# The second FFN of a decoder step by seven block products, and two residuals moved from GpSimd to VectorE

## Chip, cores and metric

One NeuronCore of a Trainium2 chip runs the whole step in one launch. The metric is the device time of that core in microseconds. A median is over three runs of the same program.

## What is computed

One inference step of a one-layer decoder: 1024 prompt rows and 32 sample rows (8 sequences of 4), D = 1024, F = 2816, all in float32.

```python
h = x + 0.5 * rms_norm(swiglu_ffn(rms_norm(x, norms[0]), f1_gu, f1_d), norms[1])
mix = token_mixer(rms_norm(h, norms[2]), ...)
h = h + rms_norm(mix, norms[3])
h = h + 0.5 * rms_norm(swiglu_ffn(rms_norm(h, norms[4]), f2_gu, f2_d), norms[5])

def swiglu_ffn(x, w_gate_up, w_down):
    gate, up = jnp.split(x @ w_gate_up, 2, axis=-1)
    return (jax.nn.silu(gate) * up) @ w_down
```

The token mixer (gated DeltaNet heads and stick-breaking heads, then `@ w_o`) is in the middle and is not touched. The two FFNs have the same shapes.

## The kernel before

**Number format.** Every large product is made of three matmuls. An operand a is split into a_hi (ScalarE rounds it to fp32r) and a_lo = a - a_hi (VectorE); the product is hi*hi + lo*hi + hi*lo, accumulated in PSUM. So every operand costs a ScalarE pass and a VectorE pass, and three matmuls, beside what it costs to load.

**Order.** Each engine's instructions are written as generators that yield times; `interleave` merges them into one program order per engine. There is no other scheduler: an instruction that waits holds up everything behind it on its engine. The times are units of a stage's own (one is a mixing tile in `second_half`).

**First FFN, `Ffn7` (line 572).** The rows lie in two parts, q = 0 (2 x 256 rows) and q = 1 (2 x 272, with the sample rows). Tokens times weights is a 2 x 2 block product, done with seven products in place of eight, which needs sums of the token blocks (t1 to t4) and of the weight blocks (s1 to s4). Four stages:

- *Head* (`head_project`, L674): the first pair of 128 wide column blocks (gate and up), without the trick: 16 products of 24 matmuls. Beside it `TokenSplit` (L1320) turns the normed rows, writes hi, a raw copy and lo, and `sums_add`, `sums_hi`, `sums_lo` make the token sums.
- *Units* (`units`, L820): 20 units, one for each remaining column block, of seven products (L815 to L817) with 24 matmuls each, 256 or 272 columns wide. The results are chained by VectorE (`dve_unit`), the hidden values' sums are stored to DRAM (`hid_rows`, `store_hidden`), and the sample rows' down product is made on the way (L792).
- *Streamed down* (`down`, L1201): 7 products over the 11 pairs of hidden blocks. Six of them are 66 steps of 12 matmuls (L1219 to L1221). Step s needs a row of hidden sums, read back from DRAM into a ring of three (`load_a`, L1050: load s waits until a_lo of step s-3 is made), its hi and lo (L1106, L1119), and the hi and lo of a 128x512 block of w_down or of a sum of such blocks (L1113, L1121). w_down's quarters lie in four slots; `step_sums` (L1123) makes their sums from step 20 on and waits for the whole slot 12.
- *Last product* (`down_last`, L1181): the seventh product, by stripes i = 0 to 3 of 33 matmuls (L1193 to L1195). Stripe i waits for u3d, the additions of the sixth product (`down_adds`).

**Mixing and the seam (`second_half`, L2172).** For nine tiles, TensorE turns `mixed` (L2325) and multiplies by w_o in two halves a tile (L2337 to L2339) into banks 4 and 5; ScalarE evacuates (L2395) and squares (L2356), VectorE scales (L2502), GpSimd adds the residual h1 (L2306), ScalarE squares again, VectorE makes the normed row (L2506). SyncE stores h2 and loads the next h1.

**Second FFN, `Ffn` (line 125).** `Turn` (L465) turns the normed rows in three thirds of 352. `head_project` (L197) makes the first group of two column blocks in 12 products of 24 matmuls. Then ten groups g: gate and up of two column blocks, each 3 x 24 matmuls of 352 columns (L192 to L194), with the down product of group g-1 between them (L300 for the samples, L289 to L291, 96 matmuls of 512 columns), added to `mixed` by VectorE (L406). `down_last` (L337) is the last group's down product. Between its additions, for the tiles in turn, ScalarE squares (L2356), VectorE scales (L2521), GpSimd adds h2 (L2314) and SyncE stores; the last two tiles are VectorE's (L2527 to L2544).

## Time and profile before

| | us |
|---|---|
| median of three runs (2561.99 to 2565.17) | 2563.99 |
| the profiled execution, its own time | 2572.63 |
| its span | 2570.9 |

The profile is of one execution. Busy time is the union of an engine's instructions; PE is TensorE's matmuls, PEld its weight loads, DVE VectorE, ACT ScalarE, POOL GpSimd, SP SyncE. PEclk is the granted share of TensorE's full clock. A row of a view gives, behind a bar, the engine's idle time before the instruction and what ended it. Names with a_ belong to the first half of the kernel, with b_ to the token mixer, with c_ to the second half.

### The profile page before, as it was taken

Reading aid. Unit: us, or ns where it says so; the run is one execution under the profiler, and the core shown is the slowest. Engines: PE = TensorE matmul, PEld = TensorE weight load, DVE = VectorE, ACT = ScalarE, POOL = GpSimd, SP = SyncE. Lnnn points to the kernel's source line nnn. Section 1 sums busy time; section 2 is a strip of 40 time slices with the busy share of each in tenths; the row PEclk is TensorE's granted clock in tenths of the full one; section 3 lists DMA queues with packets and bytes.
Section 4 is the critical chain, followed back from the end, with each engine's and each line's share of the span. In section 5 each row is a group of like instructions: output and inputs, shape, how many; then the busy total and the mean of one; then the engine's idle time right before and its main releaser. Section 6 shows DMA issues by size and latency. Waiting matters only on the chain. (4 is left out here: it accounts for less than half of the span.)

```text
span 2570.9 us, 45774 instructions
## 1 busy us (share of the span) xinstructions
PE 2419.8 (94%) x18476; PEld 2140.8 (83%) x18476; DVE 1418.0 (55%) x2368; ACT 983.1 (38%) x1786; POOL 86.7 (3%) x125
## 2 busy tenths in 40 slices
PE   7999999999999899989788888799999999999997
PEld 7999999978788788878677755578999999999995
DVE  7767666658763675665357766445433333333335
ACT  7322222244545675657445545334211111111112
POOL 0000000000000000000110000021000000000002
PEclk9999999999999999999898989899999999999999
DMA  4433333464532122211286677431311111011113
GB/s 148 139 112 122 110 122 110 158 220 130 165 115 69 45 56 56 63 48 46 65 288 202 215 245 257 145 123 52 99 50 50 49 36 45 33 49 39 43 57 108
DMA packets 232611, 275.50 MB, mean 107 GB/s; under 512 B 15737, under 2 KB 160377, under 8 KB 232464
## 3 DMA queue, kind: packets, MB, share of 16 engines
q1 hardware_dynamic: 232464, 273.45, 33.1%
q8 instruction: 103, 1.69, 0.3%
q14 instruction: 44, 0.36, 0.0%
HBM read 222.51 MB, written 50.89 MB: 106 GB/s over the span
## 5 line engine op out<-in xcount | busy, mean ns | idle before, releaser
L1546 PE MATMUL a_q<-a_uh,a_p_hi 128*128 128x352 f32 x672 | 241.4, 359 | 0.0
L1548 PE MATMUL a_q<-a_uh,a_p_lo 128*128 128x352 f32 x672 | 219.1, 326 | 0.0
L1547 PE MATMUL a_q<-a_ul,a_p_hi 128*128 128x352 f32 x672 | 218.9, 326 | 0.0
L373 ACT ACTIVATE c_hid_hi<-c_hid 128x1056 fp32r<-128x1056 f32 x20 | 21.7, 1086 | 451.6 <-DVE c_hid_samples L262 451.6
L194 PE MATMUL c_q<-c_uh,c_lo_u 128*128 128x352 f32 x528 | 170.8, 323 | 0.0
L194 PE MATMUL c_q<-c_uh,c_lo_g 128*128 128x352 f32 x528 | 170.7, 323 | 0.0
L192 PE MATMUL c_q<-c_uh,c_hi_u 128*128 128x352 f32 x528 | 170.6, 323 | 0.0
L192 PE MATMUL c_q<-c_uh,c_hi_g 128*128 128x352 f32 x528 | 170.5, 323 | 0.0
L193 PE MATMUL c_q<-c_ul,c_hi_u 128*128 128x352 f32 x528 | 170.0, 322 | 0.0
L193 PE MATMUL c_q<-c_ul,c_hi_g 128*128 128x352 f32 x528 | 170.0, 322 | 0.0
L406 DVE TENSOR_TENSOR w_mixed<-w_mixed,c_q 128x512 f32<-128x512 f32 x160 | 109.4, 687 | 104.7 <-PE c_q L291 104.7
L1546 PEld LDWEIGHTS a_q<-a_uh,a_p_hi 128*128 128x128 f32 x672 | 129.1, 192 | 28.2 <-issue 24.4
L289 PE MATMUL c_q<-c_hi_d,c_hid_hi 128*128 128x512 f32 x352 | 141.2, 401 | 3.6 <-DVE w_mixed L406 3.6
L291 PE MATMUL c_q<-c_lo_d,c_hid_hi 128*128 128x512 f32 x352 | 138.9, 395 | 0.0
L290 PE MATMUL c_q<-c_hi_d,c_hid_lo 128*128 128x512 f32 x352 | 138.7, 394 | 0.0
L1547 PEld LDWEIGHTS a_q<-a_ul,a_p_hi 128*128 128x128 f32 x672 | 129.6, 193 | 0.0
L1548 PEld LDWEIGHTS a_q<-a_uh,a_p_lo 128*128 128x128 f32 x672 | 128.5, 191 | 0.0
L423 DVE TENSOR_TENSOR c_hid<-c_silu,c_q 128x352 f32<-128x352 f32 x60 | 31.3, 522 | 174.6 <-PE c_q L194 174.6
L1219 PE MATMUL a_q<-a_b_hi,a_a_hi 128*128 128x512 f32 x264 | 104.3, 395 | 3.3 <-DVE a_a_lo L1119 3.1
L1221 PE MATMUL a_q<-a_b_lo,a_a_hi 128*128 128x512 f32 x264 | 103.7, 393 | 0.0
L1220 PE MATMUL a_q<-a_b_hi,a_a_lo 128*128 128x512 f32 x264 | 103.5, 392 | 0.0
L194 PEld LDWEIGHTS c_q<-c_uh,c_lo_g 128*128 128x128 f32 x528 | 100.2, 190 | 0.0
(618 smaller groups left out, 6510.5 us busy)
## 6 DMA issues: line engine op xcount, KB each, us to landing
b_page<-in_cache_k SPq DMA_DIRECT2D x128, 256.0 KB, 3.7
b_page<-in_cache_v SPq DMA_DIRECT2D x128, 256.0 KB, 3.7
a_w_raw<-in_ffn_gu SPq DMA_DIRECT2D x44, 512.0 KB, 5.1
a_a_raw<-hid_rows SPq DMA_DIRECT2D x66, 256.0 KB, 2.7
a_p_raw<-in_w_in SPq DMA_DIRECT2D x28, 512.0 KB, 4.0
a_raw_d<-in_ffn_d SPq DMA_DIRECT2D x11, 1024.0 KB, 4.9
hid_rows<-a_hs SPq DMA_DIRECT2D x44, 256.0 KB, 3.4
c_raw_g<-in_ffn_gu SPq DMA_DIRECT2D x11, 1024.0 KB, 5.1
```

What stands on the lines that cost most here:

```text
L192: nc.tensor.matmul(out[:, 0:TB], wh, uh[:, c, :], start=(c == 0), stop=False)
L193: nc.tensor.matmul(out[:, 0:TB], wh, ul[:, c, :], start=False, stop=False)
L194: mm = nc.tensor.matmul(out[:, 0:TB], wl, uh[:, c, :], start=False, stop=(c == KC - 1))
L289: nc.tensor.matmul(bank, hh, wh, start=(e == 0), stop=False)
L290: nc.tensor.matmul(bank, hl, wh, start=False, stop=False)
L291: mm = nc.tensor.matmul(bank, hh, wl, start=False, stop=(e == 1))
L406: self.nc.vector.tensor_tensor(to, to, self.pd[at % 2], ALU.add).then_inc(self.E("added"), 1)
L1219: nc.tensor.matmul(out[i], ah[:, cols], bh[:], start=(k == 0), stop=False)
L1221: mm = nc.tensor.matmul(out[i], ah[:, cols], bl[:], start=False, stop=(k == PAIRS - 1))
L1546: nc.tensor.matmul(self.pm[at % 2][:, 0:TB], wh, self.uh[t][:, c], start=(c == 0), stop=False)
L1547: nc.tensor.matmul(self.pm[at % 2][:, 0:TB], wh, self.ul[t][:, c], start=False, stop=False)
L1548: mm = nc.tensor.matmul(self.pm[at % 2][:, 0:TB], wl, self.uh[t][:, c], start=False, stop=(c == KC - 1))
```

## The change

The class `Ffn` is removed, and the second FFN is made by the class of the first, `Ffn7`, with a layout of its own in `second_half`. The layout tells where buffers lie, after which head products the first unit's weight buffers are free (`first_free`), which banks the head uses (four: 0, 1, 4, 5; in the first FFN six), and which banks the last product uses (those of the fifth, so that it waits for the event v and not for u3d). `TokenSplit` takes the tiles in order 0 to 8 and gets waits of its own. The output norms follow as tiles become ready: the sample tile and tiles 0 to 3 during the down phase, 4 to 7 beside the last product, each with a VectorE multiplication by the gain (while ScalarE makes the root) and a fused multiply and add of the residual; GpSimd has no part in them. In the mixing, GpSimd adds the residual for tiles 0 to 6, and VectorE, in the same fused form, for tiles 7 and 8. Some order times change, and a few semaphores of the sample's delta rule are merged, with the same counts in the same order. The first FFN's program keeps its order.

```diff
...
-class Ffn:
...
+        self.first_free, self.head_banks, self.last_banks, self.last_freed = (lay[x] for x in ("first_free", "head_banks", "last_banks", "last_freed"))
...
+                    older = i - len(self.head_banks)
+                    if older >= 0:
+                        pe.wait_ge(E("hid0" if gu else "silu0"), older // 2 + 1)
                     wh, wl = self.w0[e][gu]
-                    out = self.bank[i % 6][:, 0:WQ[q]]
+                    out = self.head_bank(i)[:, 0:WQ[q]]
...
-                    pe.wait_ge(E("u3d"), i + 1)
+                    pe.wait_ge(E(self.last_freed), i + 1)
...
+        return [self.bank[b] for b in (self.last_banks if j == 6 else (0, 1, 4, 5) if j in (0, 2, 4) else (2, 3, 6, 7))]
...
-        f = Ffn(nc, s, "f2", f_map, uh, ul, y, bank, ffn_gu, ffn_d, 103424)
+        lay = {"head": lambda q, n, size: (H0 + 32768 * q + 2 * size * n, H0 + 32768 * q + 2 * size * n + size),
...
+               "first_raw": [M0 + 28672, M0 + 36864], "first_free": [13, 14, 15, 13, 16, 15, 16], "head_banks": bank[0:2] + bank[4:6],
...
+               "kept1": M0 + 49152, "last_banks": (0, 1, 4, 5), "last_freed": "v"}
+        f = Ffn7(nc, s, "f2", whole.at, lay, quad, bank, y, ffn_gu, ffn_d, hid_rows)
...
-        turn = Turn(nc, s, "n3", uh, ul, bank[6:8], ident, lambda i: mixed[:, i, :], E("hn_ready"),
-                    [-3, -2, -1, 0.5, 1.5, 2.5, 4.5, 5.5, 6.5])
+        first_pair, second_pair = bank[6:8], bank[2:4]
+        split = TokenSplit(nc, s, "n3", f, [second_pair if z % 2 else first_pair for z in range(N)], ident,
+                           lambda z: hn_last if z == NT else mixed[:, z, :], E("hn_ready"), list(range(N)),
+                           [-3.9, -3.2, -2.2, -1.5, 0.35, 1.2, 2.0, 2.8, 3.6])
...
-        LAST = [0, NT] + list(range(1, NT))
+        LAST = [NT] + list(range(NT))
         ALL = 2 * N
-        FFN_AT, FFN_UNIT = 9.0, 0.33
+        BY_POOL = NT - 1
+        FFN_AT, FFN_UNIT = 9.0, 0.268
+        FIRST_AT = (5.9, 6.3, 6.8, 7.3)
+        TAIL_AT = [-60, -31, -24, -15, -6, 4.4, 12.0, 19.6, 27.0]
...
-                sp.wait_ge(E("w_lo"), 2 * KC)
-                f.load(sp, "g", 0)
                 sp.wait_ge(sample.E("states_out"), 16 * H_DN)
-                f.load(sp, "u", 0)
+                for e in range(2):
+                    f.load_weights(sp, 0, e)
...
-            f.load(sp, "d", 0)
-            f.load_groups(sp)
...
+            f.load_weights(sp, 1, 0)
+            sp.wait_ge(f.E("mm0"), 14)
+            f.load_weights(sp, 1, 1)
+            f.load_units(sp)
+
+            def load_h2(z):
+                sp.dma_start(res[z % 4][:], h2[TILE0[LAST[z]]:TILE0[LAST[z]] + P, :]).then_inc(E(f"res_in{z % 4}"), 16)
+
+            def tail():
+                yield -75.0
+                sp.wait_ge(f.E("mm"), 7 * UNITS_7)
+                sp.dma_start(g_end[:], norms[5].partition_broadcast(P)).then_inc(E("end_gain"), 16)
+                sp.wait_ge(E("h2_out0"), 16 * 5)
+                sp.wait_ge(E("h2_out1"), 16 * 4)
+                sp.wait_ge(f.E("hid_out"), 112 * PAIRS)
+                for z in range(4):
+                    load_h2(z)
+                for z, i in enumerate(LAST[:-1]):
+                    yield TAIL_AT[z] + 5.5
+                    sp.wait_ge(E("done"), z + 1)
+                    sp.dma_start(y_out[new_cols(i)[0], :], y[new_cols(i)[1], i, :]).then_inc(E("stored"), 16)
+                    if z + 4 < N:
+                        load_h2(z + 4)
+                for half in range(2):
+                    yield TAIL_AT[-1] + 4.0 + half
+                    cols = slice(half * 512, half * 512 + 512)
+                    sp.wait_ge(E("done"), N + half)
+                    sp.dma_start(y_out[new_cols(LAST[-1])[0], cols], y[:, LAST[-1], cols]).then_inc(E("stored"), 16)
+
+            interleave(f.load_steps(sp), f.load_last(sp), tail())
...
-                for i in range(N):
+                for i in range(BY_POOL):
...
-            pool.wait_ge(E("h_ready"), N)
             f.make_spread(pool, ident)
-            for z, i in enumerate(LAST[:-2]):
-                pool.wait_ge(E(f"res_in{z % 4}"), 16 * (z // 4) + 16)
-                pool.wait_ge(E("end_normed"), z + 1)
-                nc.gpsimd.tensor_tensor(y[:, i, :], y[:, i, :], res[z % 4][:], ALU.add).then_inc(E("done"), 1)
...
-                yield 0
-                pe.wait_ge(sample.E("new_ready"), 2 * H_DN)
-                yield from f.head_project(pe, turn.lo_half, (turn.done(2, 0), turn.done(5, 0), turn.done(NT)), (E("y_out"), ALL))
-
-            interleave(turn_mixed(), mix(), sample.multiply(pe), shifted(turn.pe(pe, ((E("m_lo"), N),)), FFN_AT, FFN_UNIT), shifted(head(), FFN_AT, FFN_UNIT))
-            f.project_groups(pe)
-            for _ in f.down_last(pe):
-                pass
+                yield -0.1
+                pe.wait_ge(E("y_out"), ALL)
+                yield from f.head_project(pe, split.lo, [split.upto(t) for t in ((0, 1), (2, 3), (4, 5, NT), (6, 7, NT))])
+
+            free = ((0, E("m_lo"), N), (1, sample.E("new_ready"), 2 * H_DN), (1, sample.E("o_out"), 1))
+            interleave(turn_mixed(), mix(), sample.multiply(pe), shifted(split.pe(pe, free), FFN_AT, FFN_UNIT), shifted(head(), FFN_AT, FFN_UNIT))
+            f.units(pe)
+            interleave(f.down(pe), f.down_last(pe))
...
+                act.wait_ge(f.E("c22d"), 4)
+                nc.scalar.activation(sq3[:, 512:D], y[:, i, 512:D], ACT.Square, accum_out=norm[:, 0, 0, 0:1]).then_inc(E("half_squared"), 1)
+                yield TAIL_AT[z]
+                event, count = f.finished(i)
+                act.wait_ge(event, count)
+                nc.scalar.activation(sq3[:, 0:512], y[:, i, 0:512], ACT.Square, accum_out=norm[:, 2, 0, z:z + 1]).then_inc(E("squared2"), 1)
...
+            ffn = (shifted(x, FFN_AT, FFN_UNIT) for x in (
+                split.act(act, ((0, E("y_mm"), FIRST), (0, sample.E("states_out"), 16 * H_DN), (4, E("y_mm"), ALL))),
+                f.head_silu(act, 2.5), f.first_unit_hi(act),
+                f.sums_hi(act, (6.0, 9.4), (((split.turned, 8),), ((split.turned, 18), (E("h2_out0"), 80), (E("h2_out1"), 64))))))
+            interleave(head_norms(), round_mixed(), round_weights(), evacuate(), second_norms(), sample.copy(act),
+                       f.head_weights_hi(act, FIRST_AT, ((0, sample.E("states_out"), 16 * H_DN), (1, E("finished"), N - EARLY_TILES))), *ffn)
+            f.act_units(act)
+            interleave(f.down_hi(act), f.last_hi_parts(act), f.down_copies(act), f.last_unit_act(act), norms_out(), last_tile())
...
+                    if i >= BY_POOL:
+                        dve.wait_ge(E("squared0"), i + 1)
+                        nc.vector.tensor_tensor(mixed[:, i, :], mixed[:, i, :], g_post[:], ALU.mult).then_inc(E("gained"), 1)
+                    yield i + 1.51 if i < NT - 1 else i + 1.72 if i < NT else i + 1.22
                     rstd = inverse(0, i)
-                    nc.vector.scalar_tensor_tensor(mixed[:, i, :], mixed[:, i, :], rstd, g_post[:], ALU.mult, ALU.mult).then_inc(E("normed"), 1)
-                    yield i + 2.38 if i < NT - 1 else i + 2.75 if i < NT else i + 2.85
+                    if i < BY_POOL:
+                        nc.vector.scalar_tensor_tensor(mixed[:, i, :], mixed[:, i, :], rstd, g_post[:], ALU.mult, ALU.mult).then_inc(E("normed"), 1)
+                    else:
+                        if i == BY_POOL:
+                            dve.wait_ge(E("h_ready"), BY_POOL)
+                        dve.wait_ge(E("gained"), i - BY_POOL + 1)
+                        dve.wait_ge(E(f"h1_in{i % 2}"), 16 * (i // 2) + 16)
+                        nc.vector.scalar_tensor_tensor(mixed[:, i, :], mixed[:, i, :], rstd, hr[i % 2][:], ALU.mult, ALU.add).then_inc(E("h_ready"), 1)
+                    yield i + 2.38 if i < NT - 1 else i + 2.0 if i < NT else i + 1.5
                     rstd = inverse(1, i)
-                    dve.wait_ge(E(f"h2_out{i % 2}"), 16 * (i // 2) + 16)
-                    nc.vector.scalar_tensor_tensor(mixed[:, i, :], mixed[:, i, :], rstd, g_pre[:], ALU.mult, ALU.mult).then_inc(E("hn_ready"), 1)
-
...
+                    if i < NT:
+                        dve.wait_ge(E(f"h2_out{i % 2}"), 16 * (i // 2) + 16)
+                    out = mixed[:, i, :] if i < NT else hn_last[:]
+                    nc.vector.scalar_tensor_tensor(out, mixed[:, i, :], rstd, g_pre[:], ALU.mult, ALU.mult).then_inc(E("hn_ready"), 1)
...
+                for z, i in enumerate(LAST[:-1]):
+                    yield TAIL_AT[z] + 1.4
+                    dve.wait_ge(E("squared2"), z + 1)
+                    nc.vector.tensor_tensor(y[:, i, :], y[:, i, :], g_end[:], ALU.mult).then_inc(E("end_gained"), 1)
+                    yield TAIL_AT[z] + 2.7
                     rstd = inverse(2, z)
-                    nc.vector.scalar_tensor_tensor(y[:, i, :], y[:, i, :], rstd, g_end[:], ALU.mult, ALU.mult).then_inc(E("end_normed"), 1)
-
...
+                    dve.wait_ge(E("end_gained"), z + 2)
+                    dve.wait_ge(E(f"res_in{z % 4}"), 16 * (z // 4) + 16)
+                    nc.vector.scalar_tensor_tensor(y[:, i, :], y[:, i, :], rstd, res[z % 4][:], ALU.mult, ALU.add).then_inc(E("done"), 1)
+
+            def last_tile():
+                z, i = N - 1, LAST[-1]
+                yield 10.0
                 dve.wait_ge(E("half_squared"), 1)
                 nc.vector.tensor_scalar(norm[:, 0, 1, 0:1], norm[:, 0, 0, 0:1], 1.0 / D, EPS, ALU.mult, ALU.add).then_inc(E("half_mean"), 1)
...
+                nc.vector.tensor_tensor(y[:, i, 512:D], y[:, i, 512:D], g_end[:, 512:D], ALU.mult).then_inc(E("end_gained"), 1)
+                yield TAIL_AT[z] + 0.2
+                dve.wait_ge(E("squared2"), N)
+                nc.vector.tensor_tensor(y[:, i, 0:512], y[:, i, 0:512], g_end[:, 0:512], ALU.mult).then_inc(E("end_gained"), 1)
+                dve.wait_ge(E("end_gained"), N + 2)
                 dve.wait_ge(E(f"res_in{z % 4}"), 16 * (z // 4) + 16)
                 rstd = inverse(2, z)
...
                 for half in range(2):
                     cols = slice(half * 512, half * 512 + 512)
-                    nc.vector.scalar_tensor_tensor(gained[0][:, cols], gained[0][:, cols], rstd, res[z1 % 4][:, cols], ALU.mult, ALU.add).then_inc(E("last_done"), 1)
+                    nc.vector.scalar_tensor_tensor(y[:, i, cols], y[:, i, cols], rstd, res[z % 4][:, cols], ALU.mult, ALU.add).then_inc(E("done"), 1)
...
-        mm.then_inc(E("g_mm"), 1)
+        mm.then_inc(E("small_mm"), 1)
...
```

## Rows read from the trace of the kernel before

**Rows 1.** The page, part 1: busy time, share of the span, instructions of each engine
```profile
PE 2419.8 (94%) x18476; PEld 2140.8 (83%) x18476; DVE 1418.0 (55%) x2368; ACT 983.1 (38%) x1786; POOL 86.7 (3%) x125
```

**Rows 2.** Busy time by stretch, second FFN: start:end length, engines, PEclk, DMA share, GB/s
```profile
1776.60:1839.50 62.90, 62.90 (x414) 62.52 (x416) 25.09 (x42) 27.40 (x49) 5.59 (x7) 1.00 0.29 95
...
2526.30:2562.40 36.10, 28.73 (x108) 18.68 (x108) 30.80 (x37) 13.46 (x27) 17.56 (x7) 0.96 0.45 149
...
2562.40:2570.90 8.50, 0.00 (x0) 0.00 (x0) 4.28 (x8) 1.02 (x3) 0.00 (x0) 0.57 0.46 185
```

**Rows 3.** Lines L192 and L300 by source: duration ns min/median/max, first to last start
```profile
L192 PEld LDWEIGHTS c_q<-c_uh,c_hi_g x528: 186/188/191, 1776.6 to 2510.9; 128*128 128x128 f32 x176
...
L300 PEld LDWEIGHTS c_q<-c_raw_d,c_hid_samples x88: 105/109/156, 1839.4 to 2526.3; 128*32 128x32 f32 x88
```

**Rows 4.** Weight loads in order of time, second FFN projection: start, us, line
```profile
1776.97 0.19 PEld L194 LDWEIGHTS c_q<-c_uh,c_lo_g 128*128 128x128 f32 x1
...
1777.45 0.19 PEld L194 LDWEIGHTS c_q<-c_uh,c_lo_g 128*128 128x128 f32 x1
```

**Rows 5.** Busy time by stretch, first FFN: head, units, streamed down, last product
```profile
25.00:72.00 47.00, 45.99 (x376) 45.31 (x375) 39.25 (x53) 31.07 (x62) 0.00 (x0) 1.00 0.13 34
...
73.00:498.50 425.50, 425.50 (x3445) 415.59 (x3444) 287.75 (x459) 121.72 (x201) 0.00 (x0) 1.00 0.38 123
...
498.50:689.30 190.80, 187.53 (x823) 151.76 (x821) 139.25 (x223) 93.76 (x167) 1.33 (x5) 0.99 0.54 174
...
694.30:730.00 35.70, 35.37 (x156) 29.05 (x157) 31.88 (x44) 18.87 (x36) 0.00 (x0) 0.92 0.63 195
```

**Rows 6.** Lines L815 and L1219 by source, first FFN
```profile
L815 PEld LDWEIGHTS a_q<-a_b11h,a_w_hi x160: 187/191/193, 73.2 to 480.4; 128*128 128x128 f32 x160
...
L1219 PEld LDWEIGHTS a_q<-a_b_hi,a_a_hi x264: 187/188/330, 498.5 to 688.6; 128*128 128x128 f32 x132
```

**Rows 7.** Weight loads in order of time: starts of down steps 20, 21, 22, 24, 59
```profile
556.64 0.19 PEld L1219 LDWEIGHTS a_q<-a_b_hi,a_a_hi 128*128 128x128 f32 x1
...
559.36 0.19 PEld L1219 LDWEIGHTS a_q<-a_b_hi,a_a_hi 128*128 128x128 f32 x1
...
565.58 0.19 PEld L1219 LDWEIGHTS a_q<-a_b_hi,a_a_hi 128*128 128x128 f32 x1 [3.54 <-DVE a_a_lo L1119]
...
572.52 0.19 PEld L1219 LDWEIGHTS a_q<-a_b_hi,a_a_hi 128*128 128x128 f32 x1
...
667.72 0.19 PEld L1219 LDWEIGHTS a_q<-a_b_hi,a_a_hi 128*128 128x128 f32 x1
```

**Rows 8.** VectorE in order of time, first FFN's down phase
```profile
562.41 0.69 DVE L1130 TENSOR_TENSOR a_slot<-a_slot,a_slot 128x512 f32<-128x512 f32 x1 [6.11 <-DMA a_slot<-in_ffn_d]
```

**Rows 9.** Who waited for whom, TensorE, 480 to 760 us
```profile
PE a_q L1193 <- DVE a_y L1275: 4.8, 1, 4.8
```

**Rows 10.** VectorE after the last matmul, in order of time
```profile
2562.39 0.67 DVE L406 TENSOR_TENSOR w_mixed<-w_mixed,c_q 128x512 f32<-128x512 f32 x1
...
2564.01 1.28 DVE L2539 SCALAR_TENSOR_TENSOR c_gained<-c_gained,c_norm_stat,c_res 128x1024 f32<-128x1024 f32 x1
...
2565.41 1.41 DVE L2544 SCALAR_TENSOR_TENSOR c_gained<-c_gained,c_norm_stat,c_res 128x512 f32<-128x512 f32 x2
```

**Rows 11.** Lines L2521 and L2153 by source: scalar_tensor_tensor of 128x1024
```profile
L2521 DVE SCALAR_TENSOR_TENSOR w_mixed<-w_mixed,c_norm_stat,c_g_end x7: 1285/2315/2326, 2535.5 to 2556.2; 128x1024 f32<-128x1024 f32 x7
...
L2153 DVE SCALAR_TENSOR_TENSOR a_y<-a_y,a_stat,a_res x9: 1284/1285/1286, 666.9 to 745.2; 128x1024 f32<-128x1024 f32 x9
```

**Rows 12.** Seam of mixing and second FFN: ScalarE timeline, chain, GpSimd group by shape
```profile
1777.01 0.60 ACT L2395 ACTIVATE w_mixed<-c_q 128x512 f32<-128x512 f32 x1 [2.95 <-PE c_q L2339]
...
1764.05 0.87 PE c_q L506 x8
...
L2306 POOL TENSOR_TENSOR w_mixed<-w_mixed,c_hr 128x1024 f32<-128x1024 f32 x9 | 22.5, 2496 | 160.4 <-DVE w_mixed L2502 160.4
```

**Rows 13.** The page, part 6: DMA issues, KB each, median us to landing
```profile
a_a_raw<-hid_rows SPq DMA_DIRECT2D x66, 256.0 KB, 2.7
```

524 lines of the change are left out of this document (105 added, 419 removed).

## The prediction

> **What bounds the kernel now.** I read the busy times first. TensorE is busy 94% of the span, its weight loads 83%, every other engine 55% or less [rows 1]. A change pays here if it takes time from TensorE's stream or from a stretch in which that stream waits. The stretches of the second FFN [rows 2] say which is which. From 1776.6 us, where its first projection starts [rows 3], TensorE is busy for all of the 62.9 us of the head. From 2526.3, where the last group's down product begins, it is busy 28.7 of 36.1 us, and from 2562.4 to the end, 8.5 us, not at all. So the stretch that the change rewrites is 2570.9 - 1776.6 = 794.3 us: almost 750 us of matmuls end to end, then a tail that VectorE sets. Everything before 1776.6 is left as it is, but for the seam.
>
> The best evidence is the first FFN, which runs the class that the second is to get, with the same counts. Its stretches [rows 5] show TensorE busy 46.0 of 47.0 us in the head, 425.5 of 425.5 in the units, 187.5 of 190.8 in the streamed down phase. I price the new second FFN from these, stage by stage, and then ask what differs.
>
> **The sum, term by term.**
>
> *Price of a projection matmul.* The units run from 73.2 us to the first down step at 498.5 [rows 6]: 425.3 us for 20 units x 7 products x 24 = 3360 matmuls of 256 or 272 columns (264 on average), and 80 small sample matmuls. Those I count at their weight load, 0.109 us [rows 3] (the same shape); that leaves 0.124 us a matmul. The old form has 352 columns and one matmul in 0.16 us: three in 0.48 [rows 4]. Old projections: 22 columns x 2 x 72 = 3168 x 0.16 = 506.9 us. New: 3360 + 384 in the head = 3744 x 0.124 = 464.3 us. Seven products for eight would save an eighth of the 20 unit columns' 460.8 us, 57.6; narrower matmuls give about a quarter of it back, and the net over all projections is 42.6.
>
> A rule speaks against the change. The Trainium skill ("TensorE: Matmul & The Clock Gate", section "Back-to-back issue gap") says that a stream of load and matmul pairs settles at about 81 ns at 128 columns and 131 ns at 512. A straight line through these, an estimate from that page, gives 99 ns at 264 columns and 110 at 352, by which the projections would cost 20 us more than before, and the whole change would bring some 23 us. The trace disagrees with both figures: 0.124 and 0.160 us [rows 4, 6].
>
> *Seam.* Four tiles instead of three are transposed inside the mixing stage, one more at 0.87 us plus its first load [rows 12], 1.0 us. New is a wait at the head's start for all 18 evacuations of the mixing, since the head now uses the two banks that the mixing accumulates in; the whole head is queued behind it. The last evacuation ran 1777.01 to 1777.61, a microsecond after the old head began [rows 12]. It now stands behind four ScalarE copies of tile 3 (0.6 each; two are new). Bounds: 1.0 us, if those copies are early, and 1.0 + 4 x 0.6 = 3.4. I take 1.5, since tile 3 is transposed well before the last half. Seam: 2.5.
>
> *Head.* 384 x 0.124 = 47.6, five transposes 5.0, and idle time as in the first FFN's head, 1.0 [rows 5]. Sum 53.6. Other engines: ScalarE gets a second copy of each transposed half (about 16 x 0.6) and eight roundings of sums (about 1.1 each): some 18 us on 27.4 in the old head [rows 2]. VectorE gets eight sums and eight remainders of 128x1024 or 1088, each like the 1.29 us of L2153 [rows 11], 21 us on 25.1. Both stay near 46 of 53.6, and the first head had VectorE at 39.3 of 47 with 1.0 us lost. Bounds for the loss: 0 and 10.
>
> *Units.* 425.3 as measured. Beside them VectorE is busy 288 us, ScalarE 122, DMA 38%. Nothing else runs in the second FFN's units either. The new waits (second raw buffer loaded after 14 head products, roundings of the first unit after products 13 to 16) have two products' slack; a 3 us miss is the bound.
>
> *Down, 66 steps.* The undisturbed step is 559.36 - 556.64 = 2.72 us, 12 matmuls at 0.227. Step 59 starts at 667.72, so 59 steps take 169.2 us where 160.5 are due [rows 6, 7]: 8.7 lost. Of that, 5.0 stand in steps 21 to 23 (572.52 - 559.36 = 13.16 against 8.16): VectorE stands 6.1 us before its first slot sum until the last quarter of slot 12 has landed [rows 8], and the remainders of step 22 are queued behind it, so TensorE waits 3.5 and then runs slow for a moment. The rest is the sample and fold matmuls. The class, its times and its loads are the same, so the stall comes back. The last seven steps had transposes of the next stage between them, which the second FFN has not: 7 x 2.72 = 19.0. Sum 188.2; bounds 183 (slot in time) and 200.
>
> *Last product.* The 4.8 us for the u3 sums [rows 9] go: the banks are now those of the fifth product, long free. What is late next is the remainder of the first stripe, 1.4 + 1.6 us on ScalarE and VectorE behind step 65's operands, some 2.6 us ahead of TensorE by the ring's depth. 4 x 33 = 132 matmuls x 0.227 = 29.9, at full clock (it was 0.92 after the wait [rows 5]). Output norms of tiles 0 to 3 fall into the last steps, about 2.6 us of VectorE each beside 1.4 us per 2.72 us step and the sums. I add 1.5 for backlog; bounds 0 and 8.
>
> *Tail.* GpSimd leaves it. With it, the 1024 wide VectorE operation took 2.3 us, without it 1.285 [rows 11]; per tile this set the old pace, and it goes wholly under the last product. After the last matmul: one addition, square, root, two halves, store. Old, from that addition: 8.5 us [rows 2]; its first half at 2565.41 stood behind the 1.28 us of the tile before [rows 10], so 1.1 less: 7.4, plus 0.3 from the last matmul: 7.7. Bounds 7 and 9.
>
> *At nothing.* Two residuals go from GpSimd (2.5 us each [rows 12]) to VectorE as one multiply and one fused add: their results are needed by transposes late in the head, and head products hide them; without this cover they would be worth 2 us each way. The merged semaphores of the sample's delta rule count the same matmuls in the same order. SyncE loads both halves of the first weights after the state stores, some 50 us before use.
>
> Sum: 2.5 + 53.6 + 425.3 + 188.2 + 29.9 + 1.5 + 7.7 = 708.7 us, against 794.3: **85.6 us less**. The profiled execution took 2572.6 us by its own time, so 2487 for one like it; it lies 8.6 over the median of the runs, 2564.0, from which I get **2478 us**.
>
> **The rivals.**
>
> *Crowded head (0.07).* ScalarE or VectorE falls behind in the head because, unlike in the first FFN, norms of the mixing's last tiles and their stores share it. The third stage of the head now needs all nine tiles, 23 us of products after its start. For it: both engines near 85%. Against: the first head lost 1.0 at 84%. Price 8 to 16 us: about 2490.
>
> *Crowded down phase (0.05).* VectorE with four output norms, twelve sums and step operands in steps 55 to 65 sets the pace. For it: 139 of 190.8 us busy in the whole phase, more at its end. Against: the first FFN had two norms a tile there and turned tiles too. Price 5 to 20: about 2490.
>
> *Weight loads as a floor (0.01).* In the units loads are busy 415.6 of 425.5 us [rows 5]. If the second FFN's matmuls paid for their loads rather than for their columns, each would keep its 0.16 us: 3744 x 0.16 = 599.0 instead of 464.3, 134.7 dearer, so slower by 49: 2613. It decides at 0.147 us a matmul. Against it stands the first FFN's 0.124 with the same operand shapes.
> The back-to-back rule of the Trainium skill named above is this rival in a milder form, with 2541 by its figures.
>
> *Row loads too slow (0.01), which ends slower.* Each down step takes back a row of hidden sums from DRAM through a ring of three; load s is issued when remainder s-3 is done. Period: (landing + 0.6 + 0.7)/3. At 2.7 us to land [rows 13] that is 1.3 us, hidden under 2.72. It decides from a step of 2.72 + 85.6/66 = 4.02 us, landing in 10.8 us. At 12 us a step is 4.4, the 66 cost 111 us more, and the time is 2589. Against: the first FFN streams the same rows at 54% DMA.
>
> *Forecast (0.86)*: its own range 2470 to 2486.
>
> **How the numbers follow.** About 0.2% (5 us) is what a measurement can tell here. The forecast and the crowded cases (0.86 + 0.07 + 0.05) are far below that line. The other two are above it, 0.02. I move 0.01 to no change, for either of these two in part: 0.97 faster, 0.01 same, 0.02 slower. The range adds the bounds below (slot in time -5, no backlog -1.5, profile to median 3) and reaches into both crowded cases: 2467 to 2494.
>
> **What would show it.** Right: no gap in TensorE's stream through 20 units of 21.3 us; down steps 2.72 apart with a single wait near step 22 on VectorE; last product without a leading wait; no GpSimd after the mixing but the spread; 7 to 8 us after the last matmul. Wrong: TensorE waiting for a b or t operand in the head (crowded head), for a remainder in the last ten steps (crowded down), or for the row loads throughout.

## The result, and the profile after

| | before | after |
|---|---|---|
| median of four runs each, on the same chip | 2564.31 | 2480.42 (2476.32 to 2485.32) |
| the profiled execution, its own time | 2572.63 | 2476.32 |
| its span | 2570.9 | 2474.6 |

The ratio is 0.9675, 95% interval 0.9656 to 0.9694: 83.9 us less, where 85.6 were forecast, and 2480.4 us where 2478 were.

The two profiled executions lie 96 us apart, more than the medians. To see what the change did, both are cut at an instruction that both have: the first transposition of the mixing. By source, that line's loads, first before and then after:

```profile
L2325 PEld LDWEIGHTS c_q<-w_ident,w_mixed x72: 135/140/231, 1631.0 to 1752.0; 128*128 128x128 f32 x64, 32*128 32x128 f32 x8
```

```profile
L2017 PEld LDWEIGHTS c_q<-w_ident,w_mixed x72: 135/140/230, 1619.4 to 1741.3; 128*128 128x128 f32 x64, 32*128 32x128 f32 x8
```

Up to there the programs do the same work, and after's execution was 11.6 us ahead. Executions scatter there: over the ten profiles of this study that have everything before that point as in the changed kernel, this first part lasted between 1619.4 and 1625.7 us, and the profiled execution of before lay 8.6 us over its median. From there to the end it is 2570.9 - 1631.0 = 939.9 us before and 2474.6 - 1619.4 = 855.2 after: **84.7 us less**. All comparisons below are of this second part or of single stages in it.

Part 1 of the page, where [rows 1] stood:

```profile
PE 2329.7 (94%) x18920; PEld 2064.0 (83%) x18920; DVE 1611.8 (65%) x2722; ACT 1097.3 (44%) x2019; POOL 63.9 (3%) x116
```

TensorE has 444 more matmuls and is busy 90 us less; VectorE is busy 194 us more and ScalarE 114 more, beside it. The share of TensorE's busy time did not move.

Where the 84.7 us come from can be added up from the distances between the starts of TensorE's matmuls in the second part, waits included. The projections took 511.3 us and take 464.4, which is 46.9 less. The down products took 251.7 us for 1056 matmuls of 512 columns and take 215.0 for 924, which is 36.7 less: the seven products save in both halves of the FFN. From the end of the last matmul to the end of the kernel it was 12.3 us and is 7.8. The stretch before the head grew by 4.9.

Busy time by stretch of the new second FFN, to be held against [rows 2, 5]: head, units, streamed down, last product, tail. The columns are the stretch and its length, busy us and instructions of PE, PEld, DVE, ACT and POOL, then PEclk, DMA share, GB/s:

```profile
1769.90:1823.00 53.10, 53.08 (x424) 53.08 (x425) 36.89 (x47) 26.38 (x51) 0.00 (x0) 0.97 0.16 44
1823.00:2248.20 425.20, 425.20 (x3441) 415.29 (x3441) 287.75 (x459) 121.69 (x201) 0.00 (x0) 1.00 0.38 123
2248.20:2436.60 188.40, 184.99 (x807) 148.76 (x806) 140.96 (x224) 91.48 (x163) 1.41 (x5) 1.00 0.56 185
2436.60:2466.40 29.80, 29.80 (x131) 24.67 (x132) 22.11 (x28) 8.99 (x14) 0.00 (x0) 1.00 0.49 161
2466.40:2474.60 8.20, 0.41 (x2) 0.00 (x0) 2.96 (x5) 1.02 (x3) 0.00 (x0) 0.76 0.17 64
```

The units repeat the first FFN's to the tenth of a microsecond, down to VectorE's 287.75. What is left over is small and stands in three places: at the head's start (the head's mean clock is 0.97), in the down phase (3.4 us without a matmul), and in the tail.

The head's start. Who waited for whom, 1764 to 1775 us (engine, line, releaser: total us, times, longest), and ScalarE in order of time (start, us, line, in brackets the idle time before and what ended it):

```profile
PEld c_q L355 <- ACT w_mixed L2087: 3.2, 1, 3.2
...
ACT c_sq L2048 <- DVE w_mixed L2207: 2.2, 1, 2.2
```

```profile
1767.91 1.06 ACT L2048 ACTIVATE c_sq<-w_mixed 128x1024 f32<-128x1024 f32 x1 [2.22 <-DVE w_mixed L2207]
...
1769.29 0.58 ACT L2087 ACTIVATE w_mixed<-c_q 128x512 f32<-128x512 f32 x1
```

The head waits 3.2 us for the last evacuation (L2087), as the new wait says it should. But the evacuation does not stand behind copies of tile 3. It stands behind the squares of tile 7, and these waited 2.2 us for tile 7's residual, which is one of the two that the change gave to VectorE.

That the squares come first is the change's own doing. The order time of ScalarE's squares is among those that it moves (NT is 8, so for tile 7 the middle one of the three values holds):

```diff
-                    yield i + 1.7 if i < NT - 1 else i + 2.2 if i < NT else i + 2.7
+                    yield i + 1.7 if i < NT - 1 else i + 1.85 if i < NT else i + 1.4
```

In the kernel before, the squares of tile 7 ran 4.8 us after the start of the last evacuation (1777.01, [rows 12]):

```profile
1781.84 1.06 ACT L2356 ACTIVATE c_sq<-w_mixed 128x1024 f32<-128x1024 f32 x1
```

After the 3.2 us gap ten head matmuls start 0.12 us apart and the next fourteen 0.21, the lower of the two clocks (1.2 GHz); the granted clock of 1769.9 to 1774.0 is 0.63.

The down phase. VectorE at step 22, where [rows 8] stood, and ScalarE shortly before step 64:

```profile
2310.89 0.69 DVE L794 TENSOR_TENSOR c_slot<-c_slot,c_slot 128x512 f32<-128x512 f32 x1 [4.86 <-DMA c_slot<-in_ffn_d]
```

```profile
2427.68 0.63 ACT L770 ACTIVATE c_a_hi<-c_a_raw 128x512 fp32r<-128x512 f32 x1 [4.00 <-DMA c_a_raw<-hid_rows]
```

The first is the stall that was forecast to come back; it costs TensorE 2.6 us here (step 21 takes 4.97 and step 22 3.05, where 2.72 are due). The second comes from SyncE's queue (the experiments without it are e9 and e12). Its waits from 2405 to 2440 us:

```profile
SPq L1984 <- DVE w_mixed L2228: 17.2, 3, 7.8
SPq L717 <- DVE c_a_lo L783: 6.2, 3, 2.4
```

SyncE stands 17.2 us in three waits before a store of a finished output tile (L1984), and the row loads of the next steps (L717) are queued behind it. Steps 63 and 64 take 3.58 and 3.73 us and the last product starts 0.4 late, 2.3 us lost by it.

The tail, where [rows 10] stood:

```profile
2466.85 0.69 DVE L942 TENSOR_TENSOR w_mixed<-w_mixed,c_q 128x512 f32<-128x512 f32 x1 [2.95 <-PE c_q L859]
...
2469.25 1.41 DVE L2244 SCALAR_TENSOR_TENSOR w_mixed<-w_mixed,c_norm_stat,c_res 128x512 f32<-128x512 f32 x2
```

VectorE idles 2.95 us before the last addition: nothing of another tile stands in front of it any more, and 7.75 us later the kernel ends.

### The profile page after: what moved, and what is told of

The parts are those of the page before. It is cut to its first block and busy times, and to the rows that moved or that the text cites. A ratio compares the mean times of both kernels' runs of the same rounds, so it can differ in the third digit from the quotient of the medians.

```text
span 2474.6 us, 47954 instructions
## 1 busy us (share of the span) xinstructions
PE 2329.7 (94%) x18920; PEld 2064.0 (83%) x18920; DVE 1611.8 (65%) x2722; ACT 1097.3 (44%) x2019; POOL 63.9 (3%) x116
## 3 DMA queue, kind: packets, MB, share of 16 engines
q8 instruction: 113, 1.85, 0.3%
## 5 line engine op out<-in xcount | busy, mean ns | idle before, releaser
L883 PE MATMUL c_q<-c_b_hi,c_a_hi 128*128 128x512 f32 x264 | 103.5, 392 | 3.3 <-DVE c_a_lo L783 1.9
L883 PE MATMUL a_q<-a_b_hi,a_a_hi 128*128 128x512 f32 x264 | 103.6, 392 | 2.2 <-DVE a_a_lo L783 2.0
L885 PE MATMUL c_q<-c_b_lo,c_a_hi 128*128 128x512 f32 x264 | 102.8, 389 | 0.0
L884 PE MATMUL c_q<-c_b_hi,c_a_lo 128*128 128x512 f32 x264 | 102.7, 389 | 0.0
L1626 DVE TENSOR_TENSOR_SCAN a_run<-a_run,a_zeros 128x1024 f32<-128x1024 f32 (+7 forms) x64 | 84.3, 1347 | 23.4 <-ACT a_run L1571 22.7
L2676 PE MATMUL b_S<-w_ident,b_page 128*128 128x128 f32 x512 | 70.1, 287 | 5.3 <-DMA b_page<-in_cache_k 3.9
L783 DVE TENSOR_TENSOR c_a_lo<-c_a_raw,c_a_hi 128x512 fp32r<-128x512 f32 x66 | 45.4, 688 | 39.9 <-ACT c_a_hi L770 39.7
L783 DVE TENSOR_TENSOR a_a_lo<-a_a_raw,a_a_hi 128x512 fp32r<-128x512 f32 x66 | 45.5, 690 | 38.7 <-ACT a_a_hi L770 38.5
L1563 ACT ACTIVATE a_ex<-a_q,a_bias 128x512 f32<-128x512 f32 (+3 forms) x96 | 50.6, 579 | 44.2 <-PE a_q L1515 36.1
L2676 PEld LDWEIGHTS b_S<-w_ident,b_page 128*128 128x128 f32 x512 | 59.0, 147 | 12.1 <-issue 7.6
L1500 DVE TENSOR_TENSOR a_ex<-a_ex,a_run 128x1024 f32<-128x1024 f32 (+7 forms) x64 | 46.1, 754 | 34.9 <-ACT a_run L1578 34.7
```

The lines of the kernel that those rows point to most:

```text
L783: nc.vector.tensor_tensor(self.a_lo[s % 3][:], self.a_raw[s % 3][:], self.a_hi[s % 3][:].bitcast(F32), ALU.subtract).then_inc(E("a_lo"), 1)
L883: nc.tensor.matmul(out[i], ah[:, cols], bh[:], start=(k == 0), stop=False)
L884: nc.tensor.matmul(out[i], al[:, cols], bh[:], start=False, stop=False)
L885: mm = nc.tensor.matmul(out[i], ah[:, cols], bl[:], start=False, stop=(k == PAIRS - 1))
L1500: self.nc.vector.tensor_tensor(x, x, self.run[m % 2][:, e, 0:self.keys(m)], ALU.mult).then_inc(self.E("weighted"), 1)
L1563: nc.scalar.activation(self.ex[m % 2][:, e, c0:c1], self.z[e][:, 0:c1 - c0], ACT.Exp, bias=self.bias[:, 2 * hp + e:2 * hp + e + 1]).then_i ...
```

## The experiments

The times of single runs scatter by more than most of these edits are worth, so the stages of the profile decide. Lengths of the second FFN's stages, worked out from the starts of the loads of L2017, L355, L479, L883 and L857 (two or three lines further on where an edit adds lines) and the end of the span:

| run | mixing to head | head | units | down | last and tail | second part | first FFN's down |
|---|---|---|---|---|---|---|---|
| after | 150.5 | 53.0 | 425.3 | 188.4 | 38.0 | 855.2 | 193.5 |
| e8_after_again | 150.9 | 53.0 | 425.3 | 189.9 | 38.0 | 857.0 | 193.7 |
| e1_seam | 148.7 | 51.5 | 425.3 | 188.6 | 38.0 | 852.1 | 193.7 |
| e2_late_sums | 151.1 | 53.1 | 425.3 | 187.9 | 38.0 | 855.3 | 190.9 |
| e3_all_pool | 153.4 | 53.8 | 425.3 | 189.3 | 38.0 | 859.8 | 193.9 |
| e4_u3d_banks | 150.9 | 53.0 | 425.3 | 191.3 | 38.0 | 858.5 | 193.5 |
| e5_ring_one | 151.2 | 53.1 | 425.3 | 248.4 | 38.0 | 915.9 | 193.6 |
| e6_narrow_units | 148.7 | 52.8 | 386.9 | 188.0 | 38.0 | 814.4 | 193.5 |
| e11_narrow_208 | 150.9 | 53.1 | 387.2 | 192.6 | 38.0 | 821.7 | 193.7 |
| e10_half_weights | 151.0 | 53.0 | 343.2 | 193.6 | 38.5 | 779.2 | 193.9 |
| e7_eighth_product | 150.6 | 53.0 | 484.3 | 188.7 | 38.0 | 914.7 | 193.9 |
| e9_three_mended | 146.9 | 51.5 | 425.3 | 189.6 | 38.1 | 851.4 | 192.4 |
| e12_early_slots | 148.6 | 51.5 | 425.3 | 183.6 | 38.1 | 847.0 | 190.9 |

The same program's down phase came out 1.5 us apart in two runs, its mixing 0.4; head, units and end repeat within 0.1. Mixing scatters by more than that: with its code untouched it is 150.5 to 151.2 us in eight profiles, but 148.7 in e6_narrow_units, as short as with e1_seam's edit. What does repeat is the time from the end of the last mixing matmul to the head's first load. It is 2.79 to 2.80 us wherever the seam is as in the changed kernel (e6 among them), 0.69 in e1, e9 and e12, and 5.27 in e3. The seam's experiments are read from that. The down phase scatters most by its step 21, which takes 3.9 to 6.6 us in the ten profiles whose sums and slot loads are untouched, and 2.72 only in e2, e9 and e12.

### The unedited kernel again (e8_after_again)

> The changed kernel again, unedited, as the measure for the run beside it. Both theories expect its median at 2480 us within 3 and its parts of the second FFN (head 53, units 425.3, down 188.3, last product 29.2) within 0.5 us of those in its first profile.

2480.37 us, ratio 0.9679 (0.9664 to 0.9693). The median and the other stages are as expected. The down phase is not: it was to be within 0.5 us of 188.3 and is 189.9, with step 6 at 3.19 us (2.72 in the first profile), step 21 at 5.53 (4.97) and step 48 at 3.57 (3.15).

### What holds the head's start (e1_seam, e3_all_pool)

```diff
-yield i + 1.7 if i < NT - 1 else i + 1.85 if i < NT else i + 1.4
+yield i + 1.7 if i < NT - 1 else i + 2.06 if i < NT else i + 1.4
 mean_square(1, i, mixed[:, i, :], E("h_ready"), i + 1, sq2)
```

> ScalarE's squares for tile 7's second norm are put behind its last evacuation of the mixing. Theory: in the changed kernel the head of the second FFN starts 3.2 us late because that evacuation stood behind those squares, and they behind VectorE's residual of tile 7; so the gap of 3.2 us before the head's first product shrinks to about 1 us, and the dozen head matmuls at half pace that followed the gap run at full pace. The stretch from the first mixing transpose to the first unit becomes 3 to 4.5 us shorter. Rival: the evacuation is late because of ScalarE's copies of tile 3 or another piece of work; then the gap keeps at least 2.5 us and the stretch loses 0 to 1 us.

ScalarE in order of time, with the squares behind the evacuation:

```profile
1773.29 0.60 ACT L2087 ACTIVATE w_mixed<-c_q 128x512 f32<-128x512 f32 x1 [1.48 <-PE c_q L2031]
1773.92 1.06 ACT L2048 ACTIVATE c_sq<-w_mixed 128x1024 f32<-128x1024 f32 x1
```

Now the evacuation waits only for the last mixing matmul. The head waits 1.1 us where it waited 3.2, and its matmuls run at full pace from the first (granted clock 1.00 where it was 0.63), so the head is 1.5 us shorter. That is 3.6 us by these rows, and the same in e9 and e12. The second part is 3.1 us shorter than in the first profile of the changed kernel and 4.9 shorter than in the second, with the scatter of mixing and down in it. The theory held.

```diff
-BY_POOL = NT - 1
+BY_POOL = N
```

> GpSimd adds the residual of all nine mixing tiles, where the changed kernel gives the last two to VectorE. Theory: the residual of tile 7 then ends later than VectorE's 1.28 us, the squares of tile 7 and the evacuation behind them with it, and the head starts another 0.7 to 3 us later than in the changed kernel. Rival: the evacuation does not depend on that residual; the head starts at the same place within 0.5 us, and only the row path of the last tile (norm, transposes, late operands) moves.

Who waited for whom, around the head's start:

```profile
PEld c_q L355 <- ACT w_mixed L2087: 5.7, 1, 5.7
...
ACT c_sq L2048 <- POOL w_mixed L2003: 4.7, 1, 4.7
```

The residual on GpSimd takes 2.34 us where VectorE takes 1.28, and starts later; the evacuation passes all of it on. From the last mixing matmul to the head it is 5.27 us, 2.5 longer, and the head is 0.8 longer. So with the changed kernel's order the move of the last residuals to VectorE, which the prediction put at nothing, is worth 3.3 us, by way of an evacuation that merely stands behind it. With the order of e1_seam, or of the kernel before, the residual is out of the evacuation's way; what the move is worth then was not tried.

### The stall at step 22 (e2_late_sums)

```diff
-yield down_time(20 + 1.5 * k) - 1.0
+yield down_time(23 + 1.4 * k) - 1.0
 self.loaded(dve, "12", k)
...
-yield down_time(36 + 0.5 * k) - 1.0
+yield down_time(38.5 + 0.5 * k) - 1.0
```

> In both FFNs VectorE's sums over the arriving step blocks are given later places in its order (three steps later for the first group, two and a half for the second). Theory: the stall of TensorE at steps 21 to 24 (2.5 us in the second FFN, 5.0 us in the first) comes from VectorE standing in its queue before a slot whose load has not landed while the remainders of the next steps are queued behind it; with the sums later, the stalls go and each down phase is shorter by them: about 5 us in the first FFN, 2.5 in the second. Rival: the sums then come too late for the units that use them and TensorE waits for VectorE elsewhere; the two phases keep their lengths within 1 us or grow. The second FFN's gaps of about 1 us near steps 58 to 65 (2.3 us in all) have another cause and stay in both cases.

The stall at step 22 is gone in both FFNs. The first FFN's down phase is 2.6 us shorter, half of what was expected: its stall is 2.7 to 2.9 us in the unedited changed kernel's two profiles, not the 5.0 that the profile of the kernel before showed. In the second FFN steps 47 and 48 now take 3.5 and 3.8 us (2.7 and 3.2 to 3.6 unedited). A likely reason is that VectorE, with the sums finished later, comes to the first output norm with work in arrears; but step 48 takes 3.8 us in e3, e4 and e7 too, where the sums were not moved, so only part of it is the edit's. The phase is 0.5 to 2.0 us shorter. Both theories hold in part: the wait goes, and some time comes back at later steps.

### The banks of the last product (e4_u3d_banks)

```diff
-"last_banks": (0, 1, 4, 5), "last_freed": "v"}
+"last_banks": (2, 3, 6, 7), "last_freed": "u3d"}
```

> The last product of the second FFN is put on the four banks that the first FFN's uses, and waits for the running sum in them as there. Theory: the wait of 4.8 us that the prediction counted as saved comes back in part; the running sum's last addition is queued among the same VectorE work as in the first FFN, so 1.5 to 5 us stand before the last product, with the down phase before it unchanged. Rival: VectorE is ahead at this point in the second FFN, since no next stage's work is in its queue; then the wait is under 0.5 us and the choice of banks saved nothing.

TensorE's waits from 2430 to 2445 us:

```profile
PE c_q L883 <- DVE c_b_lo L785: 1.5, 2, 0.7
PE c_q L857 <- DVE w_mixed L939: 1.4, 1, 1.4
```

The wait for the running sum is back, at 1.4 us. From the start of step 65 to the first load of the last product it is 4.33 us, where both profiles of the unedited kernel have 3.09. So the other banks do save a wait, and it is worth 1.2 us, not the first FFN's 4.8 [rows 9]. The whole down phase is 1.4 and 2.9 us longer than in those two profiles; what is over 1.2 lies in earlier steps (21 and 48), which scatter without an edit too.

### Row loads that are not hidden (e5_ring_one)

```diff
-at_least(sp, self.E("a_lo"), s - 2)
+at_least(sp, self.E("a_lo"), s - (self.lag if s >= 26 else 2))
```

(lag is 0 in the second FFN, 2 in the first.)

> From step 26 on, the row load of a down step of the second FFN is issued only when the remainder of the step before it is made, where the changed kernel issues it two steps ahead. Theory: with the landing of 2.7 us no longer hidden, the chain of issue, landing, ScalarE's rounding and VectorE's remainder (about 0.6 and 0.6 us) sets the step: 4.1 to 4.6 us in place of 2.82, so 50 to 70 us more over 40 steps. That is the way in which slow row loads would have shown. Rival: other slack (copies of the operands further ahead) absorbs it, and the step stays under 3.2 us, less than 15 us in all.

Tile c_a_raw, what its users idled for (us, times), and the time to land:

```profile
  DMA c_a_raw<-hid_rows: 127.2, 44
...
DMA to landing us min/median/max: 2.5/2.7/7.5
```

The down phase is 60.0 us longer than in the first profile. The median step from 28 on is 4.10 us (2.72 in the changed kernel), against 2.7 + 0.6 + 0.7 = 4.0 by the prediction's formula with a ring of one in place of three. 39 steps of 1.38 more make 54; the rest is in single longer steps, one of 8.9 us among them. So the formula by which the prediction called the row loads hidden holds within 0.1 us with nothing ahead. That three in flight divide it by three, to 1.3 us, is seen only in that the 2.72 us steps hide it.

### What a projection matmul costs (e6, e7, e10, e11)

```diff
+if self.narrow:
+    out, uh, ul = out[:, 0:P], uh[:, :, 0:P], ul[:, :, 0:P]
```

> The projection matmuls of the second FFN's units stream only the first 128 of their 256 or 272 columns (the output leaves out the rest of those columns). Theory: the price of a projection matmul goes by its columns, so it falls from 0.124 to 0.06 to 0.08 us; a unit then falls from 21.3 us to the next bound, VectorE's 14.4 us of work per unit or TensorE's 10 to 13, so the units' 425 us become 260 to 310. Rival: the matmul is held by loading its weights or by the gap between two matmuls rather than by its columns: it stays above 0.10 us and the units keep over 345 us; at 0.124 they keep 425. From the Trainium skill (TensorE: Matmul & The Clock Gate, Back-to-back issue gap), 81 ns at 128 columns would be an estimate of 112 x 20 x 0.081 x 1.3, of the order of 230 to 290 us with the other matmuls of a unit.

The units in the narrow run, and the starts of three consecutive loads:

```profile
1822.40:2209.30 386.90, 386.83 (x3443) 377.62 (x3441) 286.65 (x458) 120.48 (x201) 0.00 (x0) 1.00 0.42 135
```

```profile
1900.15 0.19 PEld L482 LDWEIGHTS c_q<-c_b11l,c_w_hi 128*128 128x128 f32 x1
1900.26 0.19 PEld L483 LDWEIGHTS c_q<-c_b11h,c_w_lo 128*128 128x128 f32 x1
1900.37 0.19 PEld L481 LDWEIGHTS c_q<-c_b11h,c_w_hi 128*128 128x128 f32 x1
```

Half the columns bring 9% of the time. TensorE stays busy throughout, so VectorE is not the bound; a matmul of 128 columns takes 0.112 us (median of the distances of starts; (386.9 - 80 x 0.109) / 3360 = 0.113). The rival won. By the Trainium skill (TensorE: Matmul & The Clock Gate, Back-to-back issue gap) it would be 81 ns; the run disagrees. (A unit has 7 x 24 = 168 matmuls and not the 112 that the expectation's estimate multiplies, but its 230 to 290 us is missed either way.)

```diff
-    out, uh, ul = out[:, 0:P], uh[:, :, 0:P], ul[:, :, 0:P]
+    out, uh, ul = out[:, 0:208], uh[:, :, 0:208], ul[:, :, 0:208]
```

> The same narrowing to 208 of 256 or 272 columns (the output leaves out the rest). The prices so far, 0.120 us at 256 columns, 0.1265 at 272, 0.160 at 352 and 0.227 at 512, lie on one line, 0.0133 us and 0.417 us per 1000 columns. Theory of a floor: 208 columns would cost 0.100 us by that line, but the 0.112 us seen at 128 columns is a floor that holds from about 236 columns down, so the matmul takes 0.112 and the units 387 us, as at 128 columns. Rival without a hard floor: the price at 128 columns has its own cause, and 208 columns cost 0.100 to 0.105 us, or bend up smoothly between 0.112 and 0.118.

```profile
1829.60:2216.80 387.20, 387.20 (x3442) 377.61 (x3442) 286.75 (x458) 120.61 (x201) 0.00 (x0) 1.00 0.42 134
```

208 columns cost what 128 cost, 0.112 us: a flat floor from 128 to 208 columns. Where between 208 and 256 it ends was not run.

```diff
+w = P
+if self.narrow:
+    out, uh, ul, w = out[0:64, 0:P], uh[:, :, 0:P], ul[:, :, 0:P], 64
 for c in range(4):
-    cols = slice(c * P, (c + 1) * P)
+    cols = slice(c * P, c * P + w)
```

> The projection matmuls of the second FFN's units stream 128 columns, as in the narrow run, and load only 64 of the 128 weight columns (the output leaves out the other hidden rows and columns). Theory: the floor of 0.112 us that the narrow run met is the time to bring in the weights, and goes by their columns: the matmul falls to 0.06 to 0.08 us and the units to VectorE's bound, 290 to 330 us. Rival: the floor is a fixed gap between two matmuls with different weights, whatever their size: the matmul stays at 0.11 us and the units at 387 us.

```profile
1823.80:2167.00 343.20, 243.61 (x3443) 227.43 (x3442) 280.14 (x456) 114.96 (x201) 1.03 (x5) 0.93 0.47 151
```

```profile
1905.57 0.13 PEld L482 LDWEIGHTS c_q<-c_t4h,c_w_hi 128*64 128x64 f32 x1
1905.63 0.13 PEld L483 LDWEIGHTS c_q<-c_t4l,c_w_hi 128*64 128x64 f32 x1
1905.69 0.14 PEld L484 LDWEIGHTS c_q<-c_t4h,c_w_lo 128*64 128x64 f32 x1
```

With 64 weight columns the same 128 columns take 0.06 us. The theory held: the floor falls with the number of weight columns. The edit halves the output's rows with them, so it does not tell the two apart, and 0.06 us is only an upper bound for the floor at 64, since 128 columns at 0.417 us per 1000 are 0.053 alone. Now TensorE is busy 244 of 343 us, VectorE 280, and TensorE waits for VectorE's chain, at a lower mean clock (0.93). Its largest wait from 1900 to 2100 us:

```profile
PE c_q L482 <- DVE c_c L671: 33.7, 12, 2.8
```

So with matmuls this cheap the units meet their next bound at 343 us, 17.2 a unit, and not at the 14.4 of VectorE's bare work.

```diff
-for q in range(2):
+for q in (0, 1, 0, 1) if self.twice and j == 6 else (0, 1):
```

> In every unit of the second FFN the seventh block product is computed twice into the same banks, so eight products are paid for and the result is the same. Theory: TensorE alone bounds the units, so each of the 20 units gets longer by that product's 2 to 3 us (16 matmuls at 0.124 us for the two projections together with their column pieces: 24 x 0.124 = 2.95), 59 us in all, within 10 %. Rival: VectorE's chain ends units as often as TensorE's matmuls; then part of the added time is hidden and the units grow by less than 40 us.

The units take 484.33 us, 59.06 more for 20 x 24 = 480 matmuls: 0.123 each. The whole price of an eighth product shows, so TensorE alone bounds the units with seven products and with eight, and the one left out is its whole price saved: 59.1 us, where the prediction had 57.6.

### Versions with the stalls taken out (e9_three_mended, e12_early_slots)

Beside e1_seam's edit, e9 (e9_three_mended) moves only the first group of sums, and some of SyncE's stores:

```diff
-yield down_time(20 + 1.5 * k) - 1.0
+yield down_time(23 + 1.4 * k) - 1.0
...
-yield TAIL_AT[z] + 5.5
+yield TAIL_AT[z] + (10.0 if z < 4 else 5.5)
```

> Three edits of order together: tile 7's squares behind the last evacuation, VectorE's first group of step sums three steps later in both FFNs (the second group stays where the changed kernel has it), and SyncE's stores of the first four finished tiles 4.5 us later, so that the row loads of the last steps no longer stand behind a store that waits for VectorE. Theory, from the parts seen so far: 3.1 us at the seam, 2.6 in the first FFN, 2.5 to 3 at step 22 of the second and 2.3 at its last steps, 10 to 11 us less than the changed kernel in all, ratio about 0.9957. Rival: the stalls are the place where the loads' or VectorE's lateness shows, and with one gone the next step stalls by as much, as in the run that moved both groups of sums; then only the seam's 3 us and the first FFN's 2.6 are kept, 5 to 6 us in all.

2473.02 us, ratio to the kernel before 0.9651 (0.9632 to 0.9669), on the same chip as the unedited kernel's 2480.37; the two intervals overlap by a little. Between the forecasts: 7.4 us by the medians, 5.6 in the second part of the profile and 1.2 in the first FFN. The seam's gain is whole and the late steps 63 and 64 are at 2.72. But in both FFNs step 38 now takes 4.35 us, where VectorE runs the end of the first group of sums straight into the second (seven sums in a row), and in the second FFN ScalarE once waited 7.8 us for a row load, which made steps 43 and 44 together 4.7 us longer:

```profile
2372.47 0.63 ACT L770 ACTIVATE c_a_hi<-c_a_raw 128x512 fp32r<-128x512 f32 x1 [7.77 <-DMA c_a_raw<-hid_rows]
```

The loads issued from 2357 to 2368 us, by tile, with KB each and median us to landing:

```profile
c_res<-h SPq DMA_DIRECT2D x4, 512.0 KB, 7.2
c_a_raw<-hid_rows SPq DMA_DIRECT2D x5, 256.0 KB, 7.5
```

The four loads of h2 for the output norms go out in 1.4 us, and the three row loads issued after them land in 10.0, 8.7 and 7.5 us instead of 2.7. The changed kernel issues the same four loads in the same 1.4 us, and its three row loads there land in 8.1, 6.8 and 4.8 us (8.4, 7.1 and 5.2 in its second profile), and no step there is longer than 2.72. So every version comes close to this stall. Whether e9's edits had a part in the longer landings is not shown, and spreading the four loads was not tried.

e12 keeps e1's and the stores' edits, leaves the sums where they were and loads the slots earlier:

```diff
-if s == 18:
+if s == 14:
     sp.wait_ge(E("sample_mm"), PAIRS)
-if 18 <= s < 22:
-    self.load_slot(sp, "21", s - 18)
-if 22 <= s < 26:
-    self.load_slot(sp, "12", s - 22)
+if 14 <= s < 18:
+    self.load_slot(sp, "21", s - 14)
+if 18 <= s < 22:
+    self.load_slot(sp, "12", s - 18)
```

> VectorE's sums keep the changed kernel's places; in their stead the loads of slots 21 and 12 are issued four steps earlier, in both FFNs. The squares of tile 7 and the stores of finished tiles stay as in the run of three edits. Theory: the stall at steps 22 and 24 is VectorE standing before the landing of slot 12, so with the landing four steps (11 us) earlier it goes without pushing VectorE's sums into the next group, and no stall comes at step 38 or 39 either: each down phase loses about 3 us, the seam 3.1, the last steps 2.3, together 10 to 12 us less than the changed kernel, a ratio to the kernel before of 0.963 to 0.964. Rival: the step is short of VectorE's time over this whole stretch, whatever the loads do; then a stall of 1.5 to 3 us comes back at some later step, and the time is that of the run of three edits (ratio 0.9651) within 1.5 us.

2465.74 us, ratio 0.9627 (0.9611 to 0.9643). The second FFN's down phase:

```profile
2239.40:2422.90 183.50, 183.50 (x806) 148.92 (x805) 142.38 (x226) 91.77 (x163) 1.40 (x5) 1.00 0.59 189
```

TensorE is busy in all of it, with the same 142 us of VectorE work, and the first FFN's is 2.8 us shorter than in e8. The second part is 10.0 us shorter than in e8 and 8.2 shorter than in the first profile. The theory held: no step after the first ten is more than 0.3 us over 2.72. VectorE had the time all along; it stood before a load that was issued too late. Against the changed kernel that is a ratio of 0.9627 / 0.9679 = 0.9946 by the medians. The two were compared through the kernel before, not side by side; their intervals do not overlap.

## Why the prediction was right

It priced a stage that the trace already held, by the same class and the same counts; so most terms could be read and not guessed. The long terms are right by their mechanism. That the total is right within 1 us is in part luck: 1.7 of the seam's +2.4 us are made up for by the head and the end, and in the down phase two errors cancel. Point by point, predicted and measured:

- **Projection matmul and units.** 0.124 us and 425.3 us; measured 425.27 in every run whose units are unedited. e7 shows that TensorE alone bounds them. That the price goes by columns held for the widths of this kernel, but only just: the price is 11% above a floor that e6 and e11 found at 0.112.
- **Seam, 2.5 us.** Mixing to head grew by 150.5 - 145.6 = 4.9, which is 0.5 over the upper bound (1.0 + 3.4 = 4.4). The end of the last mixing matmul came 1.7 us later, for the fourth tile's 1.0 and with the scatter of mixing in it, and the wait is 3.2 us, for 1.5. The size of the wait is inside its bounds, but its mechanism was another. "It now stands behind four ScalarE copies of tile 3" failed: those had ended before, and the squares of tile 7 held the evacuation. The prediction overlooked the order time (1.85 for 2.2) by which the change puts them ahead of it.
- **At nothing: the two residuals.** Failed. The step named as cover "transposes late in the head" and overlooked the residual's other reader, ScalarE's squares, queued before the evacuation that now releases the head. The order of e1_seam gives 3.6 us back by the rows of the seam and the head; e3_all_pool loses another 3.3 there.
- **Head, 53.6 us.** 53.0, for partly wrong reasons: about 1.5 us of it are the slow clock after the seam's gap (51.5 without), and no idle time was added. ScalarE and VectorE were to be busy near 46 us and were busy 26.4 and 36.9. The prediction added the new copies, roundings and sums to the old head's busy time without taking out what the old head did for its own transposed thirds and next groups. So the crowded head's "both engines near 85%" did not come about.
- **Down, 188.2 us.** 188.4 and 189.9, of other parts. The stall, predicted at 5.0 us in steps 21 to 23, cost 2.6 in the first profile and 3.2 in the second; its cause was as predicted, which e12 shows by removing it (183.5 without the late steps too, the predicted bound of 183 with the slot in time). That the total fits is luck: the 2.4 us that this is short of 5.0 came back, as 2.3, at steps 63 to 65, from SyncE's stores ahead of the row loads (with the stores later, in e9 and e12, these steps are at 2.72). That is a queue that the prediction did not follow through the steps in which the output norms had been moved. The crowded down phase was right in asking about these ten steps and wrong in the engine.
- **Last product, 29.9 + 1.5 us.** 30.2 from its first load to the end of its last matmul, without backlog. The leading wait is gone; its worth is 1.2 us here (e4) and not 4.8. A likely reason, not tested, is that VectorE had the next stage's transposed rows and norms in its queue there and has only output norms here.
- **Tail, 7.7 us.** 7.8 from the end of the last matmul, of which 7.75 from the start of the last addition, where the prediction had 7.4 and 0.3 before it. GpSimd is out of it, and the addition no longer stands behind another tile.
- **Weight loads as a floor.** The rival's form, 0.16 us whatever the columns, is refuted by 0.120 at 256 and 0.1265 at 272. A floor exists all the same, below the price and not above it. The rule of the Trainium skill (TensorE: Matmul & The Clock Gate, Back-to-back issue gap), by which the change would have brought 23 us, lost at both widths: 0.112 for its 81 ns at 128 columns, and 0.227 for its 131 ns at 512.
- **Row loads too slow.** Refuted in this kernel (median landing 2.7 us); its formula fits e5 within 0.1 us.

In sum: seam and mixing 4.9, head 53.0, units 425.3, down 188.4, the rest 38.0, 709.6 us against 708.7 predicted. The errors were +2.4, -0.6, 0, +0.2 and -1.1 us.

## What to carry to other kernels

When a stage is priced by a twin in the same trace, its long terms can be read from it, and the errors here sat at the joints: follow every queue (ScalarE's, SyncE's too) from the new wait backwards to each thing that stands before its releaser, with the change's own order times, and ask of every moved operation who all its readers are. Take a stall away by bringing forward what it waits for; putting the waiting work later, in e2 and e9, brought part of it back at other steps. And before cutting matmuls narrower still, find the floor that the weights set.
